# When a second attention normalises, when rotary low halves are made, and how far ahead the third branch loads

## The reference, cut to what matters

```python
mod = silu(c) @ w_ada[l] + b_ada[l]              # six vectors of 1024; the same for context
h   = modulate(rms_norm(x, g_mix[l]), sh1, sc1)
a_b, a_c, a_x, na_q, na_k, na_v, sw_q, sw_k, sw_v, ga, gb, gc = split_in(h @ w_in[l])
o_a = a_b * short_conv(a_c * a_x, conv_w[l])                      # first branch
o_b = neighbourhood_attention(na_q, na_k, na_v, kc_na, vc_na, na_rpb[l])   # second, 8 heads
o_c = window_attention(rope(sw_q), rope(sw_k), sw_v, kc_sw, vc_sw, sink)   # third, 8 q / 2 kv heads
x   = x + gt1 * ((sum_i sigmoid(g_i) * (o_i @ w_branch[l, i])) @ w_out[l])
x   = x + gt2 * expert_choice_ffn(modulate(rms_norm(x, g_ffn[l]), sh2, sc2), ...)  # 16 experts
```

## Time and profile before

| | |
|---|---|
| median of 3 runs | 1924.29 us (1922.08 to 1924.86) |
| profiled execution | 1919.95 us, span 1918.0 us |
| granted TensorE clock, mean | 0.962 |
| TensorE busy | 1712.4 us, 89% of the span |
| VectorE busy | 775.9 us, 40% |
| ScalarE busy | 477.0 us, 25% |
| DMA | 543.83 MB, mean 284 GB/s |

### The profile page before, as it was taken

One profiled execution on the slowest core, in us unless ns is written; L12 is line 12 of the kernel. 1 busy time (PEld: TensorE's weight loads), 2 busy tenths in 40 slices (PEclk: granted clock), 3 DMA queues, 4 the chain that ended last, 5 costly groups with the idle time before them and its releaser, 6 DMA issues.

```text
span 1918.0 us, 26482 instructions
## 1 busy us (share of the span) xinstructions
PE 1712.4 (89%) x10846; PEld 990.1 (52%) x10846; DVE 775.9 (40%) x1751; ACT 477.0 (25%) x1047; POOL 110.1 (6%) x149
## 2 busy tenths in 40 slices
PE   5999998898999899999998699989898997877775
PEld 2887776666666333333332398877693332222222
DVE  3355545554443333323232475667553221111112
ACT  3224444443123100000000344555342000000001
POOL 1002210000000100000000101300001000000000
PEclk8999999999999999999999899989899999989997
DMA  9433222113787999999999864427678999999996
GB/s 351 137 88 88 84 66 72 40 33 127 241 296 282 385 428 428 426 428 427 428 427 428 316 198 121 122 89 236 211 294 367 426 426 426 426 427 425 426 427 267
DMA packets 149875, 543.83 MB, mean 284 GB/s; under 512 B 9786, under 2 KB 92032, under 8 KB 124156
## 3 DMA queue, kind: packets, MB, share of 16 engines
q1 hardware_dynamic: 147356, 535.98, 71.0%
q0 software_dynamic: 2400, 6.16, 1.2%
HBM read 539.13 MB, written 2.98 MB: 283 GB/s over the span
## 4 chain that ended last, share of the span: by engine, by line
PE 60%; DMA 25%; DVE 8%; ACT 4%; issue 2%; SPq 0%; POOL 0%; DVEq 0%; ACTq 0%
PE bank L1958 19%; PE bank L1821 10%; PE bank L1822 9%; PE bank L1823 9%; DMA ring<-in_w_exp_down 7%; DMA ring<-in_w_exp_up 7%; DMA ring<-in_w_exp_gate 6%; DMA split_slot<-in_w_exp_gate 2%; DVE WL L1418 2%; DMA ring<-in_w_in 2%; PE bank L1932 2%; PE bank L1871 2%; PE bank L1848 2%; PE bank L1736 2%; PE bank L1858 2%
## 5 line engine op out<-in xcount | busy, mean ns | idle before, releaser
L1958 PE MATMUL bank<-ring,XEP 128*32 128x256 f32 (+1 forms) x2576 | 409.0, 620 | 30.6 <-DMA ring<-in_w_exp_up 18.0
L1821 PE MATMUL bank<-HH,WH 128*128 128x512 f32 (+1 forms) x864 | 313.7, 363 | 8.5 <-DVE WL L1418 7.1
L1822 PE MATMUL bank<-HL,WH 128*128 128x512 f32 (+1 forms) x864 | 304.0, 352 | 0.0
L1823 PE MATMUL bank<-HH,WL 128*128 128x512 f32 (+1 forms) x864 | 303.4, 351 | 0.0
L1418 DVE TENSOR_TENSOR WL<-ring,WH 128x1024 fp32r<-128x1024 f32 (+1 forms) x172 | 186.9, 1089 | 229.0 <-ACT WH L1197 228.8
L1958 PEld LDWEIGHTS bank<-ring,XEP 128*32 128x32 f32 (+1 forms) x2576 | 121.2, 130 | 287.5 <-issue 236.6
L1958 PE MATMUL bank<-ring,HIDT 128*32 128x256 f32 (+1 forms) x1264 | 160.7, 499 | 44.4 <-DMA ring<-in_w_exp_down 44.4
L1668 DVE TENSOR_TENSOR X<-X,bank 128x512 f32<-128x512 f32 x192 | 118.9, 682 | 192.5 <-PE bank L1977 100.8
L1821 PEld LDWEIGHTS bank<-HH,WH 128*128 128x128 f32 x864 | 166.4, 193 | 56.2 <-issue 30.5
L1197 ACT CAST WH<-ring 128x1024 fp32r<-128x1024 f32 (+1 forms) x172 | 157.5, 925 | 126.7 <-PE bank L1823 58.8
L1823 PEld LDWEIGHTS bank<-HH,WL 128*128 128x128 f32 x864 | 166.8, 193 | 21.4
(11 more groups left out here) (223 smaller groups left out, 1894.2 us busy)
## 6 DMA issues: line engine op xcount, KB each, us to landing
ring<-in_w_exp_gate SPq DMA_DIRECT2D x57, 2048.0 KB, 30.4
ring<-in_w_exp_up SPq DMA_DIRECT2D x53, 2048.0 KB, 32.2
ring<-in_w_exp_down SPq DMA_DIRECT2D x51, 2048.0 KB, 38.4
ring<-in_w_ada SPq DMA_DIRECT2D x48, 1024.0 KB, 7.5
ring<-in_w_in SPq DMA_DIRECT2D x40, 1024.0 KB, 5.8
split_slot<-in_w_exp_up SPq DMA_DIRECT2D x8, 2048.0 KB, 28.9
split_slot<-in_w_exp_down SPq DMA_DIRECT2D x8, 2048.0 KB, 31.6
ring<-in_w_in SPq DMA_DIRECT2D x28, 512.0 KB, 5.1
```

The source lines that it names most:

```text
L1821: mm(t, wh, hi[:, k, 0:b.n], start=k == 0, stop=False)
L1822: mm(t, wh, lo[:, k, 0:b.n], start=False, stop=False)
L1823: last = mm(t, wl, hi[:, k, 0:b.n], start=False, stop=k == b.kk - 1)
L1958: last = mm(out_bank[tw * g:tw * g + tw, 0:nw], stationary(k), w[:, g::G] if spread else w[:, nw * g:nw * g + nw], start=k == 0, stop=k == ...
```

## The change

1. In layer 0's second attention the fill is shared out unevenly: 30% of its k steps for each window pair, 20% for each context pair (10 and 6 of 32, in the last head pair 7 and 5 of 24). After two of them any pending rotary step and both normalisings are put into the list, after three the values, at 70% `lower`. Elsewhere `at_` is as before.
2. The step `split` keeps ScalarE's part (WH). VectorE's part (WL) becomes `split_low`, which follows at once, but in layer 0's second attention is held from `score` until both normalisings stand in the list.
3. The low half of the rotary step becomes a step of its own, `finish_low`, put into the list at `lower`, at the start of an attention, and ahead of the next `sk` or `sq` block's eviction.
4. The `sk` block stands before the gate pair in the fill of its head pair, and its load before theirs.
5. In the third branch, `dpair` loads a pair ahead. In layer 0 the modulation chunks alternate between a place behind the gate pair (word 3072) and slot 3 (word 12288, free once the second branch's products are done), each loaded when the chunk before it in that place is used. The loads of `w_out` are put into the last pair. In layer 1 modulation chunk 9 moves from the second attention into the third branch, with its load ahead.
6. `NWIN` is 12.

```diff
-NWIN = 8
+NWIN = 12
...
+        if b.out in ("sk", "sq"):
+            finish_low()
         P.add("done", blk=b)
...
                 P.add("finish", blk=b)
+                P.turned_low.append(b)
             P.deferred.append(rope)
+
+    def finish_low():
+        for b in P.turned_low:
+            P.add("finish_low", blk=b)
+        P.turned_low = []
...
-            per = -(-nk_atoms // len(pairs)) if nk_atoms else 0
+            early = br == "sw" and not last
             fill = list(fill)
-            for pair in pairs:
+            finish_low()
+            for n_pair, pair in enumerate(pairs):
                 P.add("score", pair=pair)
-                at_ = {-(-per * 3 // 10): values, -(-per * 9 // 20): (lambda: normalise(pair[0])), -(-per * 7 // 10): (lambda: (normalise(pair[1]), lower()))}
+                per = -(-nk_atoms // len(pairs))
+                if early:
+                    long = round(nk_atoms * 0.3)
+                    per = long if n_pair % 2 == 0 else nk_atoms // 2 - long
+                    at_ = {2: lambda: (P.flush(), normalise(pair[0]), normalise(pair[1])), 3: values, -(-per * 7 // 10): lower}
+                else:
+                    at_ = {-(-per * 3 // 10): values, -(-per * 9 // 20): (lambda: normalise(pair[0])), -(-per * 7 // 10): (lambda: (normalise(pair[1]), lower()))}
...
             P.lower = []
+            finish_low()
...
-            sums = dpair(0, p)
             if p == KB - 2:
                 sw_info, sw_atoms = qk("sw", 0)
-                sums += sw_atoms[:KD + 2]
+                atoms += sw_atoms[:KD + 2]
+            sums = dpair(0, p)
...
-                now = ((4,), (5, 6), (7,), (8, 9))[p]
+                now = ((4,), (5, 6), (7,), (8,))[p]
...
+        atoms = dpair(2, 0)
+        mods, ch = {}, []
+        homes = [(3072,), (SLOT * 3, Step(used_tile=P.tiles))]
+        if last:
+            mods[9] = mod_load(9)
+            following = dpair(2, 1)
+        else:
+            P.top = 0
+            for c in (4, 5):
+                mods[c] = mod_load(c, *homes[c % 2])
+            following = dpair(2, 1)
         for d2 in range(4):
-            atoms = dpair(2, d2)
...
+            if not last and d2 in (1, 2):
+                P.top = 0
+                following = dpair(2, d2 + 1)
+            now = 9 if last else 4 + 2 * d2
+            if now in mods:
+                ada(l, now, mods.pop(now))()
+                if d2 < 3 and not last:
+                    mods[now + 2] = mod_load(now + 2, *homes[0])
+            if not last and d2 == 3:
+                P.top = 0
+                ch = [out_load(0), out_load(1)]
...
+            if last and d2 in (0, 1):
+                atoms, following = following, dpair(2, d2 + 2)
+            else:
+                atoms = following
+            if not last:
+                ada(l, 5 + 2 * d2, mods.pop(5 + 2 * d2))()
+                if d2 < 3:
+                    mods[7 + 2 * d2] = mod_load(7 + 2 * d2, SLOT * 3, Step(used_tile=P.tiles))
...
+        def split(*blocks):
+            for b in blocks:
+                out.append(Step(kind="split", layer=l, blk=b))
+                held.append(Step(kind="split_low", layer=l, blk=b))
+            if not scored:
+                low()
...
+            if s.kind == "score" and l == 0 and s.pair[0].br == "sw":
+                scored = 2
             out.append(s)
+            if s.kind == "normalise" and scored:
+                scored -= 1
+                if not scored:
+                    low()
```

More of the change, by code:

```diff
@@ L212, in __init__ @@
         self.deferred = []
-        self.turned, self.lower = [], []
+        self.turned, self.lower, self.turned_low = [], [], []
     def add(self, kind, **kw):
@@ L574, in make_plan, with mod_load, out_load @@
         o_sw = P.obs
-        extra = [] if last else [ada(l, c) for c in (4, 5, 6, 7, 8, 9, 10, 11)]
+        def mod_load(c, home=None, free=None):
+            return [P.load([(0, (4, 512), ("w_ada", l, 512 * c, 512, 4 * r, 4))], None if home is None else home + 2048 * r, free) for r in range(2)]
+        def out_load(half):
+            return P.load([(0, (8, 512), ("w_out", l, 512 * half, 512))])
+        atoms = dpair(2, 0)
[9 more added lines that the diff above has]
+            following = dpair(2, 1)
         for d2 in range(4):
-            atoms = dpair(2, d2)
             mid = len(atoms) // 2
@@ L583, in make_plan @@
             run(atoms[1 + KD:mid])
-            if extra:
-                extra.pop(0)()
+            if not last and d2 in (1, 2):
[9 more added lines that the diff above has]
+                ch = [out_load(0), out_load(1)]
             run(atoms[mid:])
@@ L597, in make_plan @@
         ns = 1 if last else 2
-        ch = [P.load([(0, (8, 512), ("w_out", l, 512 * half, 512))]) for half in range(2)]
+        ch += [out_load(half) for half in range(len(ch), 2)]
         dense_done = Step(used_tile=stage_c_end)
@@ L680, in make_plan, with low @@
         ahead = {a.b: c for a, c in zip(layer_blocks[1:], layer_blocks[WAHEAD + 1:])}
+        scored, held = 0, []
+        def split(*blocks):
[4 more added lines that the diff above has]
+                low()
+        def low():
+            out.extend(held)
+            held.clear()
         for s in P.steps[l]:
@@ L683, in make_plan @@
             if s.kind == "k" and s.k == 0 and s.blk.b in ahead and not second:
-                out.append(Step(kind="split", layer=l, blk=ahead[s.blk.b]))
+                split(ahead[s.blk.b])
             if s.kind == "trmod" and s.k == 0:
-                out += [Step(kind="split", layer=l, blk=b) for b in layer_blocks[:2]]
+                split(*layer_blocks[:2])
+            if s.kind == "score" and l == 0 and s.pair[0].br == "sw":
+                scored = 2
             out.append(s)
+            if s.kind == "normalise" and scored:
+                scored -= 1
+                if not scored:
+                    low()
             if s.kind == "trmod" and s.k == KD - 1:
-                out.append(Step(kind="split", layer=l, blk=layer_blocks[2]))
+                split(layer_blocks[2])
             if s.kind == "done" and s.blk is layer_blocks[0]:
-                out.append(Step(kind="split", layer=l, blk=ahead[layer_blocks[1].b]))
+                split(ahead[layer_blocks[1].b])
         P.steps[l] = out
@@ L1413, in _ @@
                                                 0.5, None, ALU.mult).then_inc(cs_ready, 1)
-                    elif kind == "split":
+                    elif kind == "split_low":
                         b = s.blk
@@ L1528, in _ @@
                                 link(nc.vector.tensor_reduce(SSP[:, 0:2 * ns, b.d - 4], SQD[:, 0:2 * ns, :], AX.X, ALU.add))
+                    elif kind == "finish_low":
+                        b = s.blk
+                        dve.wait_ge(qk_hi, b.rope)
+                        if b.out == "sq":
+                            last = nc.vector.tensor_tensor(QS[b.p % 2][:, 1, 0:b.n], QT[:, 0:b.n], QS[b.p % 2][:, 0, 0:b.n].bitcast(f32), ALU.subtract)
+                        else:
+                            for hh in range(2):
+                                own = slice(64 * hh, 64 * hh + 64)
+                                for half in range(2):
+                                    last = nc.vector.tensor_tensor(dup[64 * half:64 * half + 64, 1, hh, 0:b.n], QT[own, 0:b.n],
+                                                                   dup[own, 0, hh, 0:b.n].bitcast(f32), ALU.subtract)
+                        last.then_inc(qk_ready, 1)
                     elif kind == "router_bias":
```

12 lines of the change are left out of this document (removed).

## The result

| | before | after |
|---|---|---|
| median of 4 runs each | 1923.18 us (1920.2 to 1924.86) | 1892.74 us (1887.59 to 1894.94) |
| ratio, 95% interval | | 0.9845 [0.9831, 0.9859] |
| profiled execution | 1919.95 us, span 1918.0 | 1892.0 us, span 1890.1 |
| TensorE busy | 1712.4 us | 1702.9 us |
| granted clock, mean | 0.962 | 0.965 |

The forecast was 1881 us, the range 1868 to 1905: the result lies in the range, and the forecast was 12 us too hopeful.

What follows compares the result with a forecast made beforehand. TensorE was taken to bound the dense parts, DMA the expert streams. Terms 20.8 + 5.1 + 5.4 + 5.0 + 9.0 = 45.3 us, less 2.3, gave 43 us off the 1924.29 median: 1881 us, range 1868 to 1905.

Steps and rivals of the forecast that it cites:

- The frame: Whole kernel: a microsecond taken from a dense part ends the kernel one earlier; one taken inside the expert stream gives nothing.
- the stream hides layer 0: Rival: the expert stream hides layer 0's gain, only layer 1's 14 us show; 1910 us, chance 0.06.
- C: Layer 0's third branch: earlier loads remove three of four TensorE waits for the gate; 5.4 us, bounds 3 and 6.5.
- E: Layer 1's third branch: gate weight issued before the expert load removes its wait and slow clock; 9.0 us, bounds 5 and 9.6.
- B: Layer 0's shared keys: earlier sk and separate low halves remove the 4.1 us wait; 5.1 us, bounds 2 and 7.
- A: Layer 0's second attention: waits for normalising go, 2.0 us left, and clock returns; 20.8 us, bounds 10 and 23.7.
- D: Layer 1's shared keys: the same move, with 3.0 us idle and 0.5 us clock left; 5.0 us, bounds 0 and 8.5.
- 2.3 us reserve: Whole sum: 2.3 us taken off for unfound waits from VectorE's and ScalarE's new order in some 16 unit pairs.
- waits change their name: Rival: normalising holds up weights and evictions, context pairs are too short, 20 us come back; 1901 us, chance 0.17.
- The clock doesn't return: Rival: the attention, shared-key and layer 1 third-branch gains give idle time only, 30 us; 1894 us, chance 0.08.

Runs made afterwards that it cites:

- e2: Only the third-branch part (loads a pair ahead, second home, chunk 9 moved, 12 semaphores) put into the kernel before; 1907.43 us, 0.9921.
- e3: Only the shared-keys part (sk before the gate pair, low halves as own step), with `NWIN` 12, put into the kernel before; 1917.14 us, 0.9976.
- e11: e9 with the shared keys back at the end of their head pair's fill, as before the change; 1871.79 us, 0.974 of the kernel before.
- e9: The full change with the edits of e5 and e8 together; 1865.69 us, 0.971 of the kernel before.
- e8: The full change, with WLs held in layer 0's first attention too; 1875.99 us, 0.9761 of the kernel before.
- e5: The full change, with the pending rotary step behind both normalisings in layer 0's second attention; 1880.87 us, 0.9783 of the kernel before.
- e6: The full change, but no WL is held; 1897.23 us, 0.9872 of the kernel before.
- e7: The full change, but even shares in layer 0's second attention: 8 k steps per pair, 6 in the last head pair; 1887.92 us, 0.9828 of the kernel before.
- e1: Only layer 0's second attention changed (uneven fill, early normalisings, WLs held), with `NWIN` 12, in the kernel before; 1911.4 us, 0.9944.
- e4: The full change, but with the shared keys behind the gate pair again; 1889.44 us, 0.983 of the kernel before.
- e10: e9, with layer 1's gate evicted ahead of a pending rotary step; 1867.83 us, 0.9716 of the kernel before.
- e12: e10, with WLs held in layer 1's attentions too; 1865.03 us, 0.9702 of the kernel before.

## Why the prediction was right or wrong

**The frame held.** What the dense parts gave came out at the end (15.4 us into layer 0's experts and 15.5 out; 25.9 into the last stretch and 27.9 out) within 2 us and at an unchanged rate, so the rival "the stream hides layer 0" fell. The steps add up to the difference of the spans: -4.9 + 16.0 + 6.5 - 2.2 + 0.1 + 3.1 + 7.3 + 2.0 = 27.9 us. One reading of the earlier trace rows was too simple: layer 1 has 426 GB/s, not 428, and in layer 0 TensorE is busy 100.00 of 100 us beside the full DMA engines. There the two limits stand together, and loads issued 22.8 us earlier brought the experts forward by no more than TensorE's 15.4.

**C: right.** 6.5 us measured for 5.4 (6.4 in e2). The w_out wait shrank to 0.22 us where 1 had been left. But ScalarE still waits for w_in three times (13.1 us, the longest 5.3), with TensorE covered. One of them:

```profile
501.96 1.05 ACT L1267 CAST WH<-ring 128x1024 fp32r<-128x1024 f32 x1 [4.01 <-DMA ring<-in_w_in]
```

My "9 us or more of slack" for each gate weight was therefore too generous; two blocks of weights ahead were the cover.

**E: right mechanism, one term put at nothing.** 7.3 us for 9.0. The 6.5 us wait is gone, the branch is busy 40.00 of 40 us at 1.00, and the 0.6 us that I had left at the third pair isn't there. Whether the third pair's load, now the one behind the expert transfer, was as late as the second's had been made no difference: it is due one pair later, and no cast in the branch waits for a load. The term is modulation chunk 9, "same matmuls, no gain": its product had covered a wait. Where it left, 2.15 us of idle time came (e2, and not e3); where it went, 1.9 us of work came. Without it the branch would have given 9.2 us. No run moves the chunk alone. Part of the 7.3 is the clock of this execution: e2 has the same branch at 0.96, and 5.7 us.

**B: the failed step.** "Long enough for rotary 1.3, casts 2.5 and low halves 2.8: B = 5.1 us." The result was -4.9 in this trace. I asked whether the keys would be ready in time and they were: e11 against e9 gives the place 4.8 us, nearly the 5.1. What I did not ask is what stands behind the casts on ScalarE: the gate, and the high half of the next weight. A WL waits for that high half, and on VectorE a normalising waits behind the WL. In the first attention, unlike the second, the change holds no WL; e8 shows that with the hold the 3.79 us wait goes. My lower bound of 2 us left out a loss without a reason. Some 3 of the 4.9 us are the clock of this execution (e3 reaches the same mark at 312.6 us with the same waits, last section). But the sign is no accident: the first attention took 162.1 to 165.1 us in the five kernels with early keys and no hold there (the change, e3, e5, e6, e7), and 160.3 to 160.8 in the four with late keys (before, e1, e2, e4), a loss of 1.3 to 4.8 us. Over both layers e3 against before puts keys and finish_low together at a gain of only 4.0 us.

**A: right mechanism, one term mis-sized.** 16.0 us for 20.8. The term is "I leave 2.0 us standing": 7.1 us stood. Of these 6.5 are three pairs of 1.96 + 0.22 us, from the rotary step that the change puts ahead of the normalisings. I counted the maxima, exponentials and normalising of a context pair, 3.5 us against 4.2, and not the rotary step in front of it (`P.flush()` in the diff), nor what its wait counts. e5 removes it: the attention took 122.3 us, 25.1 less than before and more than my upper bound of 23.7. The clock came back as forecast: 0.99, and 1.00 in e5 and e9.

**D: right mechanism, one term mis-sized.** 3.1 us for 5.0 (3.2 in e3). "Only some 2 us cover about 5: I leave 3.0 idle" was 4.63, so only 0.8 us of layer 1's idle time in the first attention went (7.3 to 6.5), and the rest is mostly clock (0.95 to 0.97 there). e10 shows that the gate's place isn't the whole matter: with the gate first, 4.25 of the 4.63 us come back under other names and the time doesn't move. Layer 1 has half the columns per block, and rotary, casts and low halves take about 5 us all the same. Whether more blocks between would cover them was not tried.

**What no step had.** Routing lost 2.2 us of clock, the last stretch gave 2.0. The 2.3 us reserve for unfound waits was far too small for B alone, which came out 10 us below its term. Of the rivals, "waits change their name" (1901 us) is the one that came in part: waits for a normalising kept 7.1 us, and the keys' wait moved from one queue to another. "The clock doesn't return" gave 1894 us, near the measured time, but for a wrong reason: it did return where waits went.

## What to carry to other kernels

When a step is moved off a critical queue, follow both engines' queues behind the pieces that remain: what is next after the long casts, who waits for that, and what is queued behind the one that waits. Put the urgent short work (here 0.8 us of normalising) ahead of work that may itself have to wait, a pending rotary step or a low half needed two blocks later: two such reorderings, of one line each, were worth 27 us (26 by the ratios) on top of a change of 30. But a hold pays only where nothing held is due before its release: in layer 1 the same line cost 3.9 us in the first attention and gave 3.1 in the second. And before moving a piece of work, look at what it covers where it stands: the product of chunk 9 was cover, and moving it cost its own 1.9 us.

## What the runs showed of the hardware that was not expected

The clock that TensorE gets after a wait isn't settled by the wait. The wait of 3.79 or 3.80 us that ends at 261.9 to 263.6 us stands in five executions (the change, e3, e5, e6, e7) with the same work around it. Behind it the transposes took 1.11 to 1.12 us in three of them and 0.66 us in e3 and e5. In the change 262 to 270 us was granted 0.57 (first row, busy time by stretch); the second row is e3's timeline of PE:

```profile
262.00:270.00 8.00, 6.71 (x21) 5.19 (x22) 6.17 (x12) 2.75 (x7) 0.00 (x0) 0.57 0.00 1
```

```profile
263.14 0.66 PE L1907 MATMUL bank<-CONST,PB 128*128 128x128 f32 x4 [3.79 <-DVE PB L1623]
```

From 225 us to the second attention e3 took 88 us at 0.98, the change 91 us at 0.94. The routing, where TensorE is idle in many short pieces in every kernel, was granted 1.00 before and 0.68 after. In e8 it was 1.00 again:

```profile
600.00:631.00 31.00, 24.63 (x158) 16.89 (x156) 15.46 (x49) 14.62 (x34) 5.72 (x2) 1.00 0.82 319
```

```profile
580.00:597.00 17.00, 10.95 (x88) 5.80 (x85) 11.29 (x40) 7.51 (x13) 5.72 (x2) 1.00 0.81 325
```

Over all fourteen profiles the same work, from the first matmul of the output projection to the first gather, took either 77.5 to 77.8 us (before, e4, e7, e8, e11, e12; granted 0.98 to 1.00) or 79.7 to 80.6 us (the other eight; 0.92 to 0.94). What decides this was not found. For the reading it means that 2 to 3 us of a stage's time can be the clock's of one execution; the larger terms above rest on medians of several runs or on waits that are there or not.
